# Upper halves of weights on GpSimd, and another order on ScalarE, in the gate stage of a two-block network kernel

## The reference

```python
def peer(x, w_q, sub_keys_1, sub_keys_2, u_tab, v_tab):
    ...
        v1, i1 = lax.top_k(s1, PEER_TOPK)
        v2, i2 = lax.top_k(s2, PEER_TOPK)
        ...
        top_s, pos = lax.top_k(cand_s, PEER_TOPK)
        idx = jnp.take_along_axis(cand_i, pos, axis=-1)
        g = jax.nn.softmax(top_s, axis=-1)
        u_sel = jnp.take(u_tab, idx, axis=0)
        h = jnp.einsum('bthkd,btd->bthk', u_sel, xb)
        a = (jax.nn.gelu(h.astype(jnp.float32)) * g).astype(xb.dtype)
        return jnp.einsum('bthk,bthkd->btd', a, jnp.take(v_tab, idx, axis=0))
```

## Time and profile before

| | us |
|---|---|
| median of three runs | 1819.4 |
| lowest, highest | 1818.71, 1820.29 |
| profiled execution | 1814.09 |
| its span, first to last instruction | 1812.3 |
| TensorE busy | 1685.1 |
| VectorE busy | 1191.6 |
| ScalarE busy | 892.4 |
| GpSimd busy | 304.8 |

### The profile page before, as it was taken

The page is one execution under the profiler, slowest core; times in us unless marked ns, Lnnn a source line. Parts: engine busy times, 40 slices in busy tenths (PEclk is TensorE's granted clock), DMA queues, the critical chain, the costliest instruction groups (busy, mean ns, idle before and its releaser), DMA issues.

```text
span 1812.3 us, 33301 instructions
## 1 busy us (share of the span) xinstructions
PE 1685.1 (93%) x13542; PEld 1618.4 (89%) x13542; DVE 1191.6 (66%) x2228; ACT 892.4 (49%) x1593; POOL 304.8 (17%) x174
## 2 busy tenths in 40 slices
PE   3999988899999889999899998999999999999999
PEld 3999977689999778889888998988888899999999
DVE  7666665546666666566679997777777555555554
ACT  4554433454544473444434445666666444444443
POOL 1111123211111212010057981000000000000000
PEclk9999998899999999999999999999999999999999
DMA  3555543235555433435534554444444455555553
GB/s 121 185 180 183 185 154 115 93 117 175 183 179 185 146 138 105 140 126 168 164 106 152 163 178 137 141 139 130 140 140 132 149 177 180 179 175 176 180 180 129
DMA packets 77960, 277.56 MB, mean 153 GB/s; under 512 B 9048, under 2 KB 10456, under 8 KB 77808
## 3 DMA queue, kind: packets, MB, share of 16 engines
q1 hardware_dynamic: 77808, 275.43, 46.3%
HBM read 274.35 MB, written 1.05 MB: 152 GB/s over the span
## 4 chain that ended last, share of the span: by engine, by line
PE 49%; DVE 10%; issue 2%; ACT 1%; POOL 0%; DVEq 0%; ACTq 0%
PE ps L752 49%; DVE BIG L1211 3%; DVE BIG L1626 1%; DVE BIG L1621 1%; DVE BIG L1624 1%; DVE BIG L1619 1%; DVE BIG L1622 1%; DVE WL L322 1%; DVE BIG L1658 1%; DVE BIG L1664 1%; ACT WH L466 0%; POOL MS L375 0%; DVE BIG L1656 0%; DVE XT L1211 0%; DVE MS L1211 0%
## 5 line engine op out<-in xcount | busy, mean ns | idle before, releaser
L322 DVE TENSOR_TENSOR WL<-RAW,WH 128x1024 fp32r<-128x1024 f32 x446 | 546.8, 1227 | 433.1 <-ACT WH L466 433.0
L466 ACT ACTIVATE WH<-RAW 128x1024 fp32r<-128x1024 f32 x510 | 538.1, 1057 | 588.1 <-PE ps L752 585.5
L752 PE MATMUL ps<-HH,WH 128*128 128x256 f32 x2320 | 678.8, 293 | 37.8 <-DVE HL L1211 17.8
L752 PE MATMUL ps<-HL,WH 128*128 128x256 f32 x2320 | 662.5, 286 | 0.0
L752 PE MATMUL ps<-HH,WL 128*128 128x256 f32 x2320 | 661.6, 285 | 0.0
L752 PEld LDWEIGHTS ps<-HH,WH 128*128 128x128 f32 x2320 | 450.1, 194 | 52.9 <-issue 29.1
L752 PEld LDWEIGHTS ps<-HL,WH 128*128 128x128 f32 x2320 | 451.3, 195 | 1.0 <-issue 1.0
L752 PEld LDWEIGHTS ps<-HH,WL 128*128 128x128 f32 x2320 | 451.0, 194 | 0.0
L752 PE MATMUL ps<-GH,WH 128*128 128x256 f32 x1440 | 415.9, 289 | 8.4 <-DVE GL L1211 8.4
L752 PE MATMUL ps<-GL,WH 128*128 128x256 f32 x1440 | 408.5, 284 | 0.0
L752 PE MATMUL ps<-GH,WL 128*128 128x256 f32 x1440 | 408.0, 283 | 0.0
(11 more groups left out here) (243 smaller groups left out, 1606.1 us busy)
## 6 DMA issues: line engine op xcount, KB each, us to landing
RAW<-wall SPq DMA_DIRECT2D x510, 512.0 KB, 3.5
B<-rel SPq DMA_DIRECT2D x4, 768.0 KB, 5.2
DEC<-con SPq DMA_DIRECT2D x4, 384.0 KB, 4.1
XT<-xt SPq DMA_DIRECT2D x4, 256.0 KB, 4.7
out<-XT SPq DMA_DIRECT2D x4, 256.0 KB, 2.1
NMASK<-con SPq DMA_DIRECT2D x1, 192.0 KB
CS<-con SPq DMA_DIRECT2D x1, 128.0 KB
SN<-con SPq DMA_DIRECT2D x1, 128.0 KB
```

Of the source, the lines that this page charges most:

```text
L322: ins = eng.tensor_tensor(wl, RAW[:, b % NRAW, :], wh.bitcast(F), ALU.subtract)
L466: act.activation(WH[:, b % NSPLIT, :], RAW[:, b % NRAW, :], ACT.Copy).then_inc(s_hi, 1)
L752: return pe.matmul(o, l, r, start=start, stop=stop, skip_group_check=True)
```

## The change

For blocks UP + 46 to UP + 127 (`high_on_pool`; ROUTED is 42), GpSimd makes the upper half with a `tensor_copy`, 82 in all, and tells of it by a semaphore of its own, `s_hip`. The wait of the lower half is turned to the semaphore of the engine that made the upper half. GpSimd's copy waits for the same two things as ScalarE's did: the loaded block, and the end of the block three back. On ScalarE the order in a turn becomes: gelu, upper half if it is ScalarE's, third gate terms of the quad at c - 1, copies of met units of the quad at c - 2.

```diff
+def high_on_pool(b):
+    return UP + ROUTED + 4 <= b < WP
+HIGH = []
+_made = [0, 0]
+for _b in range(N_BLOCKS):
+    _made[high_on_pool(_b)] += 1
+    HIGH.append((high_on_pool(_b), _made[high_on_pool(_b)]))
...
         def low(eng, b):
-            eng.wait_ge(s_hi, b + 1)
+            pool_made, n = HIGH[b]
+            eng.wait_ge(s_hip if pool_made else s_hi, n)
...
-            for b in range(PQ + 3, UP + ROUTED):
+            for b in range(PQ + 3, WP):
                 low_if_mine(b + 2)
+                if high_on_pool(b + 2):
+                    pool.wait_ge(d_raw[(b + 2) % NRAW], 16 * ((b + 2) // NRAW + 1))
+                    pool.wait_ge(s_blk, b)
+                    pool.tensor_copy(WH[:, (b + 2) % NSPLIT, :], RAW[:, (b + 2) % NRAW, :]).then_inc(s_hip, 1)
...
             for c in range(128):
                 if c:
                     gelu(c - 1)
+                    if not high_on_pool(UP + c + 2):
+                        high(UP + c + 2)
+                    if c - 1 in QUAD_AT:
+                        weighted(QUAD_AT[c - 1])
                     for i in range(meets_before(c - 1), meets_before(c)):
                         met(i, c)
-                    high(UP + c + 2)
-                    if c - 1 in QUAD_AT:
-                        weighted(QUAD_AT[c - 1])
```

More of the change, by code:

```diff
@@ L282, in build @@
             "d_par", "d_con", "d_inv", "d_sel", "d_mid", "d_iota", "d_key", "d_out"))
-        s_blk, s_hi, s_lo, s_lop = (sem(n) for n in ("s_blk", "s_hi", "s_lo", "s_lop"))
+        s_blk, s_hi, s_hip, s_lo, s_lop = (sem(n) for n in ("s_blk", "s_hi", "s_hip", "s_lo", "s_lop"))
         s_x, s_hh, s_hl, s_sq, s_sum, s_n1, s_ms, s_pw, s_iv, s_bc, s_rn, s_acc = (sem(n) for n in (
```

## The result

| | median us | lowest, highest | runs |
|---|---|---|---|
| before, on the same chip | 1819.1 | 1817.5, 1820.3 | 4 |
| changed | 1786.4 | 1784.9, 1792.1 | 4 |

The ratio is 0.9828, with a 95% interval of 0.9808 to 0.9848: 33 us, 1.7%, faster. The forecast was 1797.5 us in a range of 1785.5 to 1828; the time lies at its lower end, 0.9 us inside it and 11 us under the forecast.

The account below looks back on a forecast made before the run. It took a ring of waits between ScalarE and VectorE to bound the 311.4 us stretch; VectorE's queue with GpSimd's copies would then take 287 plus 3, 290 us, gaining about 22 us: 1797.5 us, range 1785.5 to 1828.

Parts of the forecast that it names:

- The ring: Gate stage, ScalarE and VectorE: upper half, lower half, gate terms, meeting, met copy wait in a circle, 4.30 us a turn.
- the 279 us that TensorE needs: Blocks 46 to 127: 81 blocks of 2.88 us plus 61 groups of gate matmuls of 0.75 us, without waits.
- rival B: Gate stage: TensorE becomes the bound, because the lock spares bf16 or copies fall into VectorE's pauses; 1787 us, chance 0.13.
- a copy adds its whole duration: VectorE's queue in the gate stage: each GpSimd copy adds 1.05 us, less what falls on a meeting or idle time.
- the sum of 287 us: Blocks 46 to 127, VectorE's queue with GpSimd's copies: 81 x (1.05 + 1.14 + 0.21) + 61 x (1.34 + 0.18).
- A's 1793 to 1804: Gate stage: copies of 0.95 to 1.2 us under the lock with VectorE, gain 26 to 15 us; chance 0.47.
- one steady turn for all: Gate stage: VectorE's turn under the lock taken as 3.74 us plus 0.18 of the meeting, P = 3.92 us.
- The mechanism of the forecast: Gate stage: VectorE together with GpSimd's copies becomes the bound, with turns of 3.9 instead of 4.3 us.
- Third gate terms ahead of the met copies: no cost: ScalarE's queue: third gate terms no longer stand behind the wait for the meeting; load about 0.4 + 1.3 + 0.3 us.
- The slower rival: VectorE's queue: copies as slow as GpSimd's other work, 81 us per us of copy, 1835 to 1893 us; chance 0.22.
- its limit of 1.45 us: Copy duration at which the predicted gain in the gate stage is zero; longer copies make the kernel slower.

Follow-up runs that it names:

- order only: Kernel before with only ScalarE's order changed: gelu, upper half, third gate terms, copies of met units; no upper halves on GpSimd; 1782.6 us, ratio 0.9806.
- upper half first: Kernel before with one swap on ScalarE: upper half ahead of the copies of met units, third gate terms still last; 1783.7 us, ratio 0.9805.
- copies up to block 105: Changed kernel, but GpSimd makes the upper halves of blocks 46 to 105 only, ScalarE those of the last 22; 1785.2 us, ratio 0.9816.
- memset: Changed kernel, but GpSimd writes zeros into the upper half where it copied; 1782.5 us in one execution.

## Why the prediction was right or wrong

**What bounds the kernel** was read rightly. The ring, its parts, and the 279 us that TensorE needs hold: the four kernels that cut the ring and in which GpSimd doesn't read beside a VectorE short of time (order only, upper half first, copies up to block 105, memset) take 278.4 to 278.7 us.

**The duration of the copy** was estimated at 1.05 us from a memset and half a subtract; undisturbed copies take 1.04. The two rows from which it was bounded were the right ones: the memset of this size takes 0.95, as its slope said.

**That GpSimd and VectorE exclude each other**, also for the bf16 gate terms, was right; rival B's first reason (it doesn't hold for bf16) fell.

**The step that was off is the charge on VectorE's queue**, "a copy adds its whole duration", 1.05 us, and so the sum of 287 us (290 with its margin). An operation that meets a copy is longer by 0.84 us (1.25 against 0.41), not 1.05: in the turn shown above it goes on at 1185.93 (its end less its own 0.41 us), 0.14 us before the copy's span ends at 1186.07. And many copies fall on a pause or a meeting. VectorE's busy time grew by 269.6 - 223.3 = 46.3 us, 0.57 us a block. With that, the same sum gives 81 x (0.57 + 1.14 + 0.21) + 61 x (1.34 + 0.43) = 263 us even with every meeting on the path, under TensorE's 279. So TensorE became the bound for most of the stretch, which was rival B by its second reason (copies in VectorE's pauses), with a chance of 0.13. The measured 1786.4 is B's 1787 and outside A's 1793 to 1804, the forecast; that it lies in the range is due to the range having been drawn down to B, not to the sum behind 1797.5. Of the signs named ahead, gate groups 3.63 us apart (B's) came up to block 106, and groups 3.9 us apart only from there; VectorE at its old durations (B's too) did not come. The rows ahead of the prediction held the smaller charge: the subtract that met GpSimd's started 0.23 us behind it, when 2.23 of its 2.46 us were left, and was longer by 2.09; I saw the exclusion in it and not its size. I also took one steady turn for all, though three turns in thirteen have no gate terms and let VectorE catch up.

**The mechanism of the forecast holds at the end of the stage.** From block 107 on, VectorE with the copies is the bound, with turns of up to 4.2 us, for the reason given; it costs 3.6 us, where the forecast had 11 over the whole stretch.

**"Third gate terms ahead of the met copies: no cost"** was right and too little: beside the copies on GpSimd it is worth 12 of the 29.2 us, since it lets VectorE be late. That the upper half's move ahead of the met copies would give the whole gain on ScalarE as well, and 3.5 us more, stands nowhere in the prediction. The ring was there to be read, but each part of the change was costed only together with the others.

**The slower rival** did not come to pass, since the copy stayed well below its limit of 1.45 us. That it had the right place, the doubled copies show: two take 2.1 us together, VectorE's queue is the bound, and the kernel is 27 us slower than before. Its price was too high: its sum gives 81 x 3.45 + 82 + 3 = 364 us for that, where 338.4 were measured.

## What to carry to other kernels

When two engines with time to spare wait for each other, look for the instruction in a queue that stands behind a wait that it doesn't need, and move it ahead; that cost nothing here, where moving the work to a third engine had a price. Before a change with several parts is judged, cost each part without the others. A GpSimd operation that reads SBUF holds up VectorE's operations with two SBUF inputs, and costs time where VectorE has no pauses to spare; the price is seen in the lengths of VectorE's own operations, not in GpSimd's idle time.

## What the runs showed of the hardware

- GpSimd's `tensor_copy` of 128 x 1024 float32 to float32r takes 1.04 us undisturbed, its memset of the same size 0.95 us, and its subtract with two inputs 2.35. The Trainium skill's "roughly line-rate" for one input (GPSIMD Engine Reference, Engine selection) is borne out, at 1.04 us against the 0.85 that I had estimated by it.
- A VectorE operation with two SBUF inputs that meets such a copy is longer by 0.84 us, the same for bf16 (0.41 to 1.25); beside the memset none is longer.
- Of the changed kernel's 82 copies, 70 take up to 1.35 us: those that meet a gate-term operation wait for that one. Eleven take 1.43 to 2.14 us, most of them begun in a lower half. One, the first, takes 3.44 us (1104.50, begun with a lower half; the next meeting of VectorE is at 1106.96). In the kernel with doubled copies one took 3.16 us. GpSimd first, then VectorE:

```profile
1133.80 3.16 POOL L473 CAST WH<-RAW 128x1024 fp32r<-128x1024 f32 x1 [3.08 <-PE ps L771]
```
```profile
1133.51 1.21 DVE L334 TENSOR_TENSOR WL<-RAW,WH 128x1024 fp32r<-128x1024 f32 x1
1134.64 0.41 DVE L1230 TENSOR_TENSOR OH<-RB,IREP 128x512 bf16<-128x512 bf16 x1
1134.98 0.41 DVE L1230 TENSOR_TENSOR XT<-RB,IREP 128x512 bf16<-128x512 bf16 x1
1135.31 0.75 DVE L1230 TENSOR_TENSOR XT<-OH,RB 128x512 bf16<-128x512 bf16 x2
1135.98 0.35 DVE L1230 TENSOR_TENSOR BIG<-BIG,ps 128x200 f32<-128x200 f32 x1
```

The copy was ready during a lower half, and four more operations of VectorE ran at full speed ahead of it; counting its 1.04 us back from its end, it got its turn at the meeting, 1135.98, which reads PSUM. So the two don't always take turns one by one. When they do and when not, these runs don't tell.
